# Expert weights loaded two units at a time, and a layer's last unit out of its turn: a two-layer encoder trunk with experts, on one core

## What is computed

```python
xt = rmsnorm(x)                                    # 256 x 1024
g_idx = argmax(softmax(xt @ group_w + group_b))    # one of 4 groups
top_p, top_i = top_k(softmax(xt @ expert_w[g_idx] + expert_b), 2)   # 2 of its 8 experts
comb = p_group * top_p / sum(top_p)
for g in range(4):                                 # all 32 experts, weights read in full
    a = einsum('nd,edf->nef', xt, w_gate[g])       # 1024 -> 256
    u = einsum('nd,edf->nef', xt, w_up[g])
    act = silu(a) * u * comb[:, g]
    y += einsum('nef,efd->nd', act, w_down[g])     # 256 -> 1024
```

## Time and profile before

| what | value |
|---|---|
| median of 3 runs | 648.47 us (647.62 to 649.98) |
| the profiled execution's own time | 648.46 us |
| its span | 646.7 us |
| TensorE busy | 577.7 us, 89% |
| TensorE's mean granted clock | 0.960 |
| HBM read | 231.67 MB |

### The profile page before, as it was taken

How to read it: one execution, slowest core, us unless ns; L and a number is a source line. 1 busy time by engine, 2 the same in 40 slices (tenths; PEclk the granted TensorE clock), 3 DMA queues, 4 the chain that set the end, 5 groups by cost and what they waited for, 6 DMA issues and landing times.

```text
span 646.7 us, 12057 instructions
## 1 busy us (share of the span) xinstructions
PE 577.7 (89%) x4992; PEld 412.4 (64%) x4992; DVE 220.1 (34%) x747; ACT 137.3 (21%) x355; POOL 6.1 (1%) x25
## 2 busy tenths in 40 slices
PE   9999999999999688585999999999999969868795
PEld 8888776885566365252768876788566636525373
DVE  4334455172232122020426687417223212202031
ACT  3143445331101000000131365513110100000011
POOL 0100000000000000000010000000000000000000
PEclk9999999999999999698999999999999998969899
DMA  8999935199999999999999992309999999999995
GB/s 328 423 418 417 416 123 195 29 421 361 420 420 420 419 420 422 421 420 422 419 417 420 422 416 101 131 25 399 381 420 420 421 420 418 420 422 421 422 419 204
DMA packets 37935, 233.61 MB, mean 361 GB/s; under 512 B 4208, under 2 KB 4336, under 8 KB 11760
## 3 DMA queue, kind: packets, MB, share of 16 engines
q1 hardware_dynamic: 34992, 227.49, 86.0%
q10 hardware_dynamic: 2880, 5.24, 2.3%
HBM read 231.67 MB, written 1.05 MB: 360 GB/s over the span
## 4 chain that ended last, share of the span: by engine, by line
PE 66%; DMA 19%; DVE 5%; issue 4%; SPq 3%; ACT 3%; DVEq 0%; ACTq 0%
PE banks L1028 13%; PE banks L770 13%; DMA ring<-in_moe_w_down 8%; PE banks L1019 7%; PE banks L859 7%; PE banks L1076 6%; PE banks L1086 6%; DMA shared<-in_moe_w_up 4%; DMA ring<-in_moe_w_up 4%; SPq L637 3%; PE banks L745 2%; PE banks L809 2%; PE banks L837 2%; DMA desk<-in_bias 2%; PE banks L826 2%
## 5 line engine op out<-in xcount | busy, mean ns | idle before, releaser
L1028 PE MATMUL banks<-ring,desk 128*32 128x256 f32 x1408 | 107.8, 389 | 16.0 <-DMA shared<-in_moe_w_up 9.8
L770 PE MATMUL banks<-ring,hT 128*128 128x256 f32 x416 | 94.6, 382 | 0.0
L1028 PEld LDWEIGHTS banks<-ring,desk 128*32 128x32 f32 x1408 | 56.7, 112 | 50.0 <-issue 24.4
L770 PEld LDWEIGHTS banks<-ring,hT 128*128 128x128 f32 x416 | 77.3, 190 | 13.2 <-issue 3.6
L1019 PE MATMUL banks<-desk,hT 128*128 128x128 f32 x512 | 64.8, 287 | 10.9 <-issue 10.2
L1076 PE MATMUL banks<-ring,desk 128*32 128x512 f32 x416 | 60.2, 679 | 15.0 <-DMA ring<-in_moe_w_down 10.7
L1019 PEld LDWEIGHTS banks<-desk,hT 128*128 128x128 f32 x512 | 63.5, 202 | 13.7 <-issue 13.1
L859 PE MATMUL banks<-heads,ring 128*128 128x256 f32 x256 | 61.8, 387 | 1.0 <-ACT heads L1217 1.0
L859 PEld LDWEIGHTS banks<-heads,ring 128*128 128x128 f32 x256 | 46.4, 190 | 13.6 <-issue 6.6
L1086 PEld LDWEIGHTS banks<-desk 128*128 128x128 f32 x224 | 41.4, 190 | 17.2 <-issue 12.1
L1086 PE MATMUL banks<-desk 128*128 128x256 f32 x224 | 52.1, 386 | 0.0
(11 more groups left out here) (183 smaller groups left out, 632.4 us busy)
## 6 DMA issues: line engine op xcount, KB each, us to landing
ring<-in_moe_w_down SPq DMA_DIRECT2D x58, 1024.0 KB, 27.0
ring<-in_moe_w_gate SPq DMA_DIRECT2D x46, 1024.0 KB, 27.2
ring<-in_moe_w_up SPq DMA_DIRECT2D x42, 1024.0 KB, 27.2
shared<-in_moe_w_up SPq DMA_DIRECT2D x20, 1024.0 KB, 23.4
ring<-in_ab_w_in SPq DMA_DIRECT2D x8, 1024.0 KB, 18.1
xT<-in_moe_w_gate SPq DMA_DIRECT2D x6, 1024.0 KB, 24.5
ring<-in_c_w_in SPq DMA_DIRECT2D x6, 1024.0 KB, 23.2
desk<-in_bias ACTq DMA_DIRECT2D x16, 256.0 KB, 7.9
```

The source lines that it names most:

```text
L770: ins = pe.matmul(bank2(SLAB_BANK[layer][s], NT)[:, t, :], hT[:, c, t * P:(t + 1) * P], w[:, c, :], start=(c == 0 and t == 0), stop=(c == ...
L1028: ins = pe.matmul(bank((4, 0)[stage])[j * SLOTS:(j + 1) * SLOTS, 0:DFF], gathered[:, c, j * SLOTS:(j + 1) * SLOTS], w[:, c, :], start=(c = ...
```

## The change

Four things change.

1. Two neighbouring units of a stage (k and k + 1, k even, from k = 16 to k = 87) are loaded by one DMA of 2 MB with a row of 16 KB in each partition, where both go to neighbouring slots that come free with the same stage. The arrays of expert weights lie in HBM in that form. In each layer the plan finds 29 such pairs: all of k = 20 to 85 but 38, 39, 42, 43, 62, 63, 66 and 67. The units that come in parts are now k = 24 to 27, two pairs, so 2 DMAs a part and not 4, with the same lengths of rows.
2. The last unit, k = 95, goes to the slot `xT` and is issued between k = 23 and k = 24; `xT` holds nothing else in the layer. The unit in halves is now k = 94.
3. `last_outputs` takes the last expert's down first: up 0, up 1, add 0, up 2, add 1, up 3, add 2, add 3, down 3, down 0, combine 3, down 1, combine 0, first half of down 2, combine 1, second half of down 2, combine 2. No down starts before all four hidden values are there.
4. The router has fewer instructions in its chain: the norm's division by `D` is done by the squares, two pairs of instructions become one form with a scalar (one instruction for each half of the tokens), and the difference for the group's softmax is taken after the pick. The idle matmuls are 11 and not 14.

```diff
-HALVED = [first_unit(l, "experts") + PER_ROUND - 1 for l in range(2)]
+AHEAD = [first_unit(l, "experts") + PER_ROUND - 1 for l in range(2)]
+HALVED = [n - 1 for n in AHEAD]
+IN_TWOS = range(4 * STAGE, PER_ROUND - 2 * STAGE)
...
+        def place(units, slots, was):
+            parted = all(w in PARTED for w in was)
+            signals[slots[0]] += len(PART_ENDS) if parted else 1
+            for n, s, w in zip(units, slots, was):
+                where[n] = (s, slots[0], signals[slots[0]], w)
+                k = n - experts
+                done = n if k < 0 or k >= PER_ROUND - STAGE else experts + k // STAGE * STAGE + STAGE - 1
+                (high if s >= LOW else free)[s] = (experts - 0.5 if outs <= n < experts else done, n)
+            order.append(units)
...
+            if AHEAD[layer] not in where and may[one][0] >= experts:
+                place((AHEAD[layer],), (STREAM,), ("stream",))
+                del high[STREAM]
+                continue
+            twos = [s for s in may if s + 1 in may and s + 1 != LOW and s + 1 < STREAM and may[s][0] == may[s + 1][0]]
+            if k in IN_TWOS and k % 2 == 0 and twos:
+                two = min(twos, key=lambda s: (may[s][0], s))
+                if may[two][0] == may[one][0]:
+                    place((n, n + 1), (two, two + 1), (may[two][1], may[two + 1][1]))
...
+            def load(units, src):
+                for n in units:
+                    wait_free(n)
+                signal = s_unit[WHERE[units[0]][1]]
...
+                sp.dma_start(ring_of(units[0], len(units)), src).then_inc(signal, 16)
...
-                down(0)
                 add_up(3)
-                down(1)
+                down(3, 0, 1)
+                down(0, 0, 1)
+                combine(3)
+                down(1, 0, 1)
                 combine(0)
-                down(2)
+                down(2, 0)
                 combine(1)
+                down(2, 1)
                 combine(2)
-                down(3)
-                combine(3)
...
-                link(V.tensor_tensor(mean[:, :], token_ss[:, :, 0], token_ss[:, :, 1], ALU.add))
-                link(V.tensor_scalar(mean[:, :], mean[:, :], 1.0 / D, EPS, ALU.mult, ALU.add))
+                link(V.scalar_tensor_tensor(mean[:, :], token_ss[:, :, 0], EPS, token_ss[:, :, 1], ALU.add, ALU.add))
...
-                V.tensor_tensor(G[4], lg, over(S[0], GROUPS), ALU.subtract).then_inc(s_rd, 1)
-                link(V.tensor_tensor(G[0], lg, over(S[0], GROUPS), ALU.is_equal))
-                link(V.tensor_tensor(G[1], G[0], rev4, ALU.mult))
+                for t in range(NT):
+                    ins = V.scalar_tensor_tensor(G[1][:, t, :], lg[:, t, :], S[0][:, t:t + 1], rev4, ALU.is_equal, ALU.mult)
+                link(ins)
...
+def in_twos(w):
+    return np.ascontiguousarray(w.reshape(EXPERTS, 2, P, UNIT).transpose(0, 2, 1, 3)).reshape(2, EXPERTS // 2, P, 2 * UNIT)
```

More of the change, by code:

```diff
@@ L149, in place_units @@
         until = (("attention", "attention", "pairs", "norms"), ("attention", "norms", "attention", "norms"))[layer]
[L150 to L162, removed]
@@ L163, in place_units @@
-    return where
-WHERE = place_units()
+        since = {"norms": outs - 0.9, "pairs": outs - 0.8, "attention": outs - 0.5}
+        high = {LOW + i: (since[what], what) for i, what in enumerate(until)}
+        high[ATTENDED] = (experts - 0.5, "attended")
+        order = []
+        def place(units, slots, was):
[7 more added lines that the diff above has]
+            order.append(units)
@@ new lines, in place_units @@
+        n = first_unit(layer, "in")
+        while n < AHEAD[layer]:
+            k = n - experts
+            may = {**free, **high} if 0 <= k < PER_ROUND - LOW else free
+            one = min(may, key=lambda s: (may[s][0], any(may.get(b, (None,))[0] == may[s][0] for b in (s - 1, s + 1)), s))
+            if AHEAD[layer] not in where and may[one][0] >= experts:
[7 more added lines that the diff above has]
+                    place((n, n + 1), (two, two + 1), (may[two][1], may[two + 1][1]))
+                    n += 2
+                    continue
+            place((n,), (one,), (may[one][1],))
+            n += 1
@@ L169, in hybrid_moe_kernel @@
+        orders.append(order)
+    return where, orders
+WHERE, LOADS = place_units()
 def hybrid_moe_kernel(nc, xT_d, small_d, bias_d, rope_d, ab_in, ab_out, c_in, c_out, gate_d, up_d, down_d, out_d):
@@ L175, in sem @@
             return ctx.enter_context(nc.semaphore(name))
-        low = [sb(f"ring{i}", [P, UNIT]) for i in range(LOW)]
+        low = sb("ring", [P, LOW * UNIT])
         shared = sb("shared", [P, HIGH * UNIT])
@@ L651, in _, with expert_unit @@
                     sp.dma_start(rope_all, rope_d[:, :]).then_inc(s_rope, 16)
[L652 to L659, removed]
                 weights = (gate_d, up_d, down_d)
-                def expert_unit(k):
-                    return weights[k % PER_BATCH // STAGE][layer, BATCH * (k // PER_BATCH) + k % STAGE]
+                experts = first_unit(layer, "experts")
+                def expert_unit(k, count=1):
+                    e, j = divmod(BATCH * (k // PER_BATCH) + k % STAGE, 2)
+                    return weights[k % PER_BATCH // STAGE][layer, e][:, j * UNIT:(j + count) * UNIT]
                 def load_round(rd):
```

130 lines of the change are left out of this document (73 added, 57 removed).

## The result

The changed kernel took **650.0 us** (median of 20 runs, 648.04 to 651.37), the one before 648.35 us (20 runs, 646.58 to 649.98). The ratio is 1.0025 with an interval of [1.0015, 1.0035]: slower by 1.65 us. The forecast was 647.5 us, a gain of 1.0. The result lies inside the range and within 0.5% of before, but it moved the other way.

The account below looks back on a forecast made before the run. Taken as the bound: DMA landings at about 420 GB/s up to unit 83, plus TensorE's work behind it. 2 x (2.50 - 2.26 - 0.70) + 0.45 - 0.51 = -1.0 us gave 647.5 us, range 643.0 to 652.0.

Parts of the forecast that it names:

- Part 1: Expert stream: the last unit ahead puts one more unit before unit 83's landing, +2.50 us a layer.
- Part 2: Stream start to unit 83: 24 pairs with fewer packets save 0.094 us each, -2.26 us a layer.
- Part 3: Router and loads in parts: shorter chain and fewer part loads start the stream sooner, -0.70 us a layer.
- Part 4: Last batch: gap before down(3), +0.45 us in layer 0; with two short waits gone, -0.51 in layer 1.
- A: Expert loads: rows of 16 KB move no faster, the unit ahead is paid in full, 652.0 us; chance 0.20.
- B: Expert loads: the packet's cost goes altogether on the pairs, 0.188 us each, 643.0 us; chance 0.15.
- C: TensorE's wait for unit 83: cut so the clock stays at 2.4 GHz, 4.1 us more go, 643.4 us; chance 0.10.
- D: Layer ends: landings of the last units bound them after all, 4 us a layer gained, 640.5 us; chance 0.05.
- the likeliest case: Whole kernel: time within 0.5% (3.2 us) of before, about what a measurement can tell from none; chance 0.50.

Follow-up runs that it names:

- late: Changed kernel, but xT takes unit 24 first, in its turn, and the last unit behind it, issued between units 83 and 84: 646.92 us, ratio 0.9978.
- noahead: Changed kernel with the last unit in its turn and the old order of the last batch; pairs and new router stay: 645.77 us, ratio 0.9962.
- late4: late with pairs only from k = 28 on, so that all parts are single: 645.68 us, ratio 0.9969.
- parts4: Changed kernel with its first pair at k = 28, so units in parts are loaded each by themselves: 648.24 us, ratio 0.9998.
- nopairs: Changed kernel with every expert unit in a DMA of its own again, rows of 8 KB: 652.83 us, ratio 1.0066.
- rows8: Changed kernel with each pair still one DMA, but of 256 rows of 8 KB instead of 128 of 16 KB: 652.66 us, ratio 1.0067.

## Why the prediction failed, by its own steps

**Part 1 (the unit ahead) was right in place and, by the landings, in size.** +2.50 us a layer was forecast, and the landings have 2.48 from unit to unit. late lies 0.47% or 3.1 us under the changed kernel. Two layers should give 5.0; its 1,680 more packets, 105 on each engine at 9 ns (last section), take 0.9 back, and the 1.0 left is within the uncertainty of 1.2 us. noahead lies 0.63% or 4.1 us under. The comparison without joined parts gives less: late4 lies 0.29% or 1.9 us under parts4, 2.8 with what its 1,584 more packets take back, uncertain by 1.3. Its waits end 2.95 and 4.89 us sooner than those of parts4, what layer 0 hands on included, which is the full price; why the medians show less is open.

**Part 2 (pairs) was right in kind, a little large.** 0.094 us a pair was taken; the landings give 2.08 / 24 = 0.087 and 1.87 / 24 = 0.078. Both are inside the rounding's 0.068 to 0.119. Reckoned in the same way against nopairs, which has as many units ahead, the pairs give 1.63 and 1.74 us, 0.07 us a pair. The packets themselves can be measured in the traces: one of 16 KB most often took 611 ns, of 8 KB 309, a small one 9 ns. Eight rows and a small packet fewer on each engine give 8 x (2 x 309 - 611) + 9 = 65 ns a pair; the medians, 613 and 312 ns, give 97. The 16 ns from the two queues were as loose as the text said.
The Trainium skill, DMA: Bandwidth & Descriptors, section on why small descriptors are slow, gives about 3 cycles a packet, from which the prediction had 3.5 ns and 0.03 us a pair. These traces show 9 ns and 0.07 to 0.09 us, and the 4.4 us between nopairs and parts4, 0.09 us a pair, agree with them within their uncertainty.

**Part 3 (the start of the stream) is the first step that failed.** I took -0.70 us a layer, 0.5 of it from the router and 0.2 from the smaller number of part DMAs. Measured: -0.48 and +0.45, 1.4 us more than forecast in the two layers. (a) "They are half as many" was counted as a gain, and was none. I had priced a DMA of two units' parts like one of one unit's. It takes SyncE 0.61 us, not 0.43, and, what counts, what it carries lands later: from first issue to last part nothing was gained in layer 0 and 0.54 us lost in layer 1. parts4 puts the form of the parts at 1.8 us for both layers (uncertain by 1.2), where I had -0.4. Why a part load over two units lands later these runs do not say; its rows are as many and as long. (b) The router's chain gave 0.30 us in layer 0 and 0.06 in layer 1, not 0.5 and 0.5; up to the matmul of the picks it was 0.3 in both, which the 0.48 of layer 0 hides. Merging two instructions into one for each half of the tokens saved 0.1 us and nothing, where I had counted 0.18 and 0.1, and in layer 1 a stall of 0.46 us on VectorE, not there before, took most of the rest. The other 0.17 us of layer 0's -0.48 stood before the router began, and were luck.

**A term was missing, the lag, and that is the second step.** I had read a unit as landed when its bytes had gone at 420 GB/s, and so put the spread of the engines at nothing. It is landed when the slowest of 16 engines is done. From the start to unit 83 the lag grew by 0.35 us more than before in layer 0, 0.91 in layer 1, 1.3 in all. What of this is the change's own stays open: between two executions of the same changed kernel this growth was 0.5 us apart in layer 0 and 1.4 in layer 1.

Neither step alone turns the sign. With the start as forecast the profiled span would still be 1.1 us longer than before, with the lag as before 1.2. Without both it would be 0.1 us shorter, and the other 0.9 us to the forecast are the pairs, 0.6, and small differences at and behind the waits.

**Part 4 (the last batch's order) was right.** The gap before `down(3)` is 0.32 us, 0.45 were forecast. Both short waits of layer 1 went. The chain behind the wait is +0.33 and -0.25 us for +0.45 and -0.51. The clock gave some of it back in layer 0: the first 32 matmuls took 6.02 us for 6.34. Without that the chain would be 0.65 longer, of which the gap is 0.32 us; in layer 1 the same 32 matmuls took 5.25 for 5.07. In both layers 0.2 to 0.3 us are left over, and in the timeline they lie between the split `down(2)` and the combines that now alternate with it; no run takes them apart.

**That pairs must wait for two slots cost nothing, as forecast.** The DMA engines were busy to the end, and the window also has TensorE's granted clock, 0.76 for 0.94:

```profile
292.00:302.00 10.00, 6.00 (x68) 3.71 (x68) 0.42 (x1) 0.66 (x2) 0.00 (x0) 0.76 1.00 424
```

**The rivals.** A had the right direction and the wrong mechanism: rows of 16 KB are faster, as nopairs and rows8 show. But what it says of the size, "It decides from a saving of under 0.07 us a pair", was the warning: the sum hung on two large terms of opposite sign, 5.0 and 4.5 us, and 0.7 us at the start. B would have needed 0.188 us a pair. C: the clock did not stay at 2.4 GHz; TensorE still waited 3.24 us and its 32 matmuls took 6.02 us, most of the way to the 1.2 GHz level. D: no wait for a last unit bounds the end.

So no difference over 0.5% came, as the likeliest case had it, and the sign did not. That the time lies in the stated range says little for the working, as two large terms cancel in it.

## What to carry to other kernels

When a stream of loads bounds a stage, find the unit whose landing ends the last long wait and count the units ahead of it. What was moved forward past it here cost its full transfer time at that landing, 2.48 us, though it filled an idle slot; move such a unit to just behind that landing. Longer rows were worth some 0.07 to 0.09 us per 2 MB while the queue stayed full. Where it had run dry and started again, loads over two units at once landed later than twice as many over one (1.8 us for two starts, uncertain by 1.2): join loads where the queue is already full. And before adding up terms of a few tenths, look at how far two executions of one kernel lie apart in them.

## What the runs showed of the hardware that was not expected

**A load lands with its slowest engine, and the engines drift apart.** At the end of the loads in parts the 16 engines end within 1.5 to 3.2 us of each other, at unit 83 within 3.4 to 5.6, in all twelve profiled executions of the eleven kernels. The lag grows in steps of about 1 us, for instance from 3.54 to 4.85 between units 62 and 63 in layer 0 after. Steps of this size stand where the DMA engines also carry the program's own fetches of instructions. The page counts these in a queue of their own:

```profile
q8 instruction: 43, 0.70, 0.4%
```

They are 16 KB each and took 1.07 us in the median, 0.89 to 1.26 us, in this trace. In the twelve executions, between the start of a stream and unit 83, the lag grows by more than 0.7 us from one load to the next 34 times. All 34 times a fetch ran between the first engine's end with the load before and the landing; of all 964 loads there, 589 have one. Most of the 287 fetches are followed by no such step, and the traces do not say which engine carried one. The Trainium skill, Runtime: NRT & Kernel Launch, section on instruction fetch, says that instructions come in blocks of 16 KiB through a DMA queue of the engine's own and that the cost is mostly hidden. The trace agrees with the size, 0.70 MB / 43. That the cost is hidden it does not bear out for this stream, which takes every engine's whole time: the steps are as long as a fetch. That the fetches cause them is argued from where they stand and was not tested, as no kernel here had fewer fetches.

**A packet's own cost on a hardware queue.** Packets of 2, 8 and 16 KB most often took 84, 309 and 611 ns, one of the semaphores 9 ns: 9 ns plus the bytes at 27.3 GB/s on each of 16 engines describes the first three within 2 ns. Nine times 9 ns are 0.081 us, which lies within the 0.07 to 0.09 us measured for a pair.
